# An expert layer's results kept on chip in pairs of experts and combined by one-hot matmuls, with two changes of order ahead of it

## The reference, cut to what matters

```python
x = x + mix @ w_out[l]
h2 = rms_norm(x, norm2_g[l])
# top-1 group of 8 experts, then top-2 experts in it; 32 experts, hidden width 512
for e in range(N_EXPERTS):
    hid = silu(t @ w_gate[e]) * (t @ w_up[e])
    y = y + gates[:, e:e + 1] * (hid @ w_down[e])
x = x + y
```

## Time and profile before

| what | value |
|---|---|
| median of 3 runs | 1212.26 us (1211.14 to 1212.79) |
| profiled execution, its own time | 1212.39 us |
| its span, first to last instruction | 1210.5 us |
| PE busy / PEld busy | 1067.1 us / 693.5 us |
| DVE / ACT / POOL busy | 434.3 / 325.5 / 285.8 us |
| mean granted TensorE clock | 0.955 of 2.4 GHz |
| DMA over the span | 278.12 MB, mean 230 GB/s |

### The profile page before, as it was taken

The page is one execution under the profiler, slowest core; times in us unless marked ns, Lnnn a source line. Parts: engine busy times, 40 slices in busy tenths (PEclk is TensorE's granted clock), DMA queues, the critical chain, the costliest instruction groups (busy, mean ns, idle before and its releaser), DMA issues.

```text
span 1210.5 us, 14085 instructions
## 1 busy us (share of the span) xinstructions
PE 1067.1 (88%) x5550; PEld 693.5 (57%) x5550; DVE 434.3 (36%) x792; ACT 325.5 (27%) x572; POOL 285.8 (24%) x189
## 2 busy tenths in 40 slices
PE   5999999999999999999989599898888878778881
PEld 4779899766698788888868333332333222223320
DVE  3332792699940443469963500100000000000003
ACT  5344632433332655522232111111101011011000
POOL 6333334332333544444330100000000000000002
PEclk8999999999999999999999699999899999998996
DMA  7222242322227222253265889999999999999966
GB/s 178 73 53 72 68 105 71 95 62 70 70 53 243 68 59 64 66 195 104 69 278 200 303 310 411 416 406 414 416 410 417 415 414 403 413 407 416 420 266 215
DMA packets 125966, 278.12 MB, mean 230 GB/s; under 512 B 12688, under 2 KB 98720, under 8 KB 109536
## 3 DMA queue, kind: packets, MB, share of 16 engines
q1 hardware_dynamic: 115584, 254.18, 56.8%
q0 software_dynamic: 4560, 12.83, 3.1%
q10 hardware_dynamic: 5776, 10.49, 2.3%
HBM read 264.95 MB, written 14.62 MB: 231 GB/s over the span
## 4 chain that ended last, share of the span: by engine, by line
PE 61%; DMA 28%; DVE 6%; ACT 2%; issue 2%; SPq 1%; POOL 0%; POOLq 0%; DVEq 0%; ACTq 0%
DMA arena<-w_exp_up_in 24%; PE bank L471 14%; PE bank L492 12%; PE bank L826 11%; PE bank L719 7%; PE bank L839 4%; PE bank L778 3%; DVE work L1295 2%; DMA arena<-w_in_in 2%; PE bank L675 1%; PE bank L658 1%; DMA x_rows<-arena 1%; PE bank L545 1%; DVE piece_r L1408 1%; DVE arena L1297 1%
## 5 line engine op out<-in xcount | busy, mean ns | idle before, releaser
L1671 POOL TENSOR_TENSOR piece_r<-arena,piece_r 128x1024 fp32r<-128x1024 f32 x84 | 201.9, 2410 | 337.4 <-ACT piece_r L903 337.3
L826 PE MATMUL bank<-arena,work 128*64 128x512 f32 x1024 | 240.5, 625 | 40.1 <-DMA arena<-w_exp_up_in 38.9
L471 PE MATMUL bank<-piece_r 128*128 128x512 f32 x936 | 232.5, 399 | 2.3 <-ACT arena L937 2.3
L471 PEld LDWEIGHTS bank<-piece_r 128*128 128x128 f32 x936 | 171.0, 188 | 42.9 <-issue 9.6
L826 PEld LDWEIGHTS bank<-arena,work 128*64 128x64 f32 x1024 | 76.0, 144 | 202.1 <-issue 196.1
L1573 DVE SCALAR_TENSOR_TENSOR work<-bank,slot_rs,work 128x256 f32<-128x256 f32 x32 | 15.5, 484 | 449.2 <-ACT work L1137 449.2
L492 PEld LDWEIGHTS bank<-piece_r 128*128 128x128 f32 x1344 | 162.0, 192 | 6.1 <-issue 6.1
L492 PE MATMUL bank<-piece_r 128*128 128x256 f32 x1344 | 164.9, 284 | 0.0
L839 PE MATMUL bank<-arena,work 128*64 128x512 f32 x512 | 128.5, 648 | 15.1 <-ACT work L1139 15.1
L1735 POOL DMA_INDIRECT arena<-x_rows,idx_all x32 | 29.6, 925 | 461.0 <-PE bank L816 389.5
L903 ACT ACTIVATE piece_r<-arena 128x1024 fp32r<-128x1024 f32 x84 | 88.5, 1056 | 139.0 <-DMA arena<-w_in_in 83.4
(11 more groups left out here) (238 smaller groups left out, 920.7 us busy)
## 6 DMA issues: line engine op xcount, KB each, us to landing
arena<-w_exp_gate_in SPq DMA_DIRECT2D x32, 2048.0 KB, 32.6
arena<-w_exp_up_in SPq DMA_DIRECT2D x32, 2048.0 KB, 39.8
arena<-w_exp_down_in SPq DMA_DIRECT2D x32, 2048.0 KB, 37.9
arena<-w_in_in SPq DMA_DIRECT2D x68, 512.0 KB, 3.9
y_rows<-work ACTq DMA_DIRECT2D x64, 96.0 KB, 6.9
arena<-w_branch_gla_in SPq DMA_DIRECT2D x8, 512.0 KB, 4.1
arena<-w_branch_dsa_in SPq DMA_DIRECT2D x8, 512.0 KB, 5.0
arena<-w_out_in SPq DMA_DIRECT2D x2, 2048.0 KB, 12.5
```

Source lines behind the costliest of these rows:

```text
L471: last = mm(bank[n % 2][:, :], w[:, k, :], h[:, k, :], start=(i == 0 and k == 0), stop=(i == 2 and k == K - 1))
L826: last = mm(bank[0][hf * WIDE:(hf + 1) * WIDE, :], hTe[sl][:, k, :], wgu[sl][2][:, :, k, hf * HALF:(hf + 1) * HALF], start=(k == 0), stop= ...
L1671: Q.tensor_tensor(quarter(w_lo, q), quarter(w_raw, q), quarter(w_hi, q).bitcast(F32), ALU.subtract).then_inc(s["wlo_ready"], 1)
```

## The change

1. **Experts in pairs.** The slots of two experts fill 128 partitions (64 each, 48 used). `idx_pair` has 16 columns, GpSimd issues 16 gathers of 128 rows into two buffers (an unused slot's index is out of bounds and moves nothing). TensorE transposes a pair at a time: eight 128x128 transposes in banks 4 and 7, after the first expert's `gate_up`. VectorE evicts each expert's half in two operations.
2. **Results stay on chip.** A slot's gate weight is multiplied into the hidden product's scale (`slot_sc`). `down` swaps the halves of bank 1 for the second expert of a pair, so that the results of two experts fill 128 partitions for each half of the columns. ScalarE writes their high parts (two copies of 64x512), VectorE their low parts (two subtractions). VectorE makes a one-hot matrix `pick` (slots x 512 tokens) for each half of the columns, by comparison with an iota.
3. **Combine.** For each of 4 blocks of tokens and 2 halves of the columns TensorE multiplies `pick` by the high and then the low part (two fp32r matmuls 128x512) into bank 2, 3 or 6, and VectorE adds the bank to x. Four tiles of the pair before stand in every expert, behind `gate_up` (and the pair's transposes) and ahead of the hidden transposes. The last pair's eight tiles come at the end.
4. **Gone:** `y_rows` with its stores, its zeroing and the two waits for that, and the eight gathers of the end. SP and ScalarE store the output in eight pieces of 256 KB, in turn.
5. **Loops written out** on all engines in the expert stage. The table of extra tiles holds a token and its gate weight.
6. **Mend one:** `split_hi(0)` in place of `split_hi(1)` ahead of the first evictions.
7. **Mend two:** the high passes of output tiles 0 to 3 run first, with k outside; the other passes follow tile by tile. ScalarE's exps are released before the last `place`.

```diff
-            for n in range(2 * T):
-                hf, t = divmod(n, T)
-                for i, (m, w) in enumerate(((mix_hi, wout_hi[hf]), (mix_lo, wout_hi[hf]), (mix_hi, wout_lo[hf]))):
...
+            for k in range(K):
+                for n in range(T):
+                    out_pass(n, 0, [k])
             for n in range(2 * T):
                 hf, t = divmod(n, T)
+                for i in range(1 if hf == 0 else 0, 3):
+                    out_pass(n, i, range(K))
...
             def gather_transposes(b, done):
                 for k in range(K):
-                    last = tr(bank[4][:, k * WIDE:(k + 1) * WIDE], xg[b].rearrange("p (q k) -> p k q", k=K)[0:WIDE, k, :],
-                              ident[0:WIDE, 0:WIDE])
+                    last = tr(bank[4 + k // 4 * 3][:, k % 4 * P:(k % 4 + 1) * P],
+                              xg[b].rearrange("p (q k) -> p k q", k=K)[:, k, :], ident[:, :])
...
+            def combine_tile(onto, picked, hi, lo, t, done):
+                mm(onto, picked[:, t * P:(t + 1) * P], hi, start=True, stop=False)
+                mm(onto, picked[:, t * P:(t + 1) * P], lo, start=False, stop=True).then_inc(done, 1)
+            def combine(p, hf):
+                pe.wait_ge(s["pick_ready"], 2 * p + hf + 1)
+                pe.wait_ge(s["y_lo_ready"], 4 * p + 4 if hf else 4 * p + 3)
+                for t in range(T):
+                    c = TILES * p + T * hf + t
+                    if c >= 3:
+                        pe.wait_ge(s["x_added"], c - 2)
+                    combine_tile(bank[COMB_BANKS[c % 3]][:, :], pick[hf], y_hi[p % 2][hf], y_lo[p % 2][hf], t, s["comb_ps"])
...
+            for e in range(NE):
+                sl, (p, q) = e % 3, divmod(e, 2)
+                pe.wait_ge(wgu_loaded[sl], 32 * (e // 3 + 1))
+                pe.wait_ge(s["he_ready"], e + 1)
+                gate_up(sl, q, s["gu_ready"])
+                if q == 0 and p + 1 < PAIRS_E:
+                    pe.wait_ge(s["he_ready"], e + 2)
+                    pe.wait_ge(xg_loaded[(p + 1) % 2], 16 * ((p + 1) // 2 + 1))
+                    gather_transposes((p + 1) % 2, s["xg_T"])
+                if p >= 1:
+                    combine(p - 1, q)
+                pe.wait_ge(s["hid_ready"], e + 1)
+                hidden_transposes(s["hidT_ps"])
+                pe.wait_ge(s["hidT_ready"], e + 1)
+                pe.wait_ge(wdn_loaded[sl], 16 * (e // 3 + 1))
+                if e >= 1:
+                    pe.wait_ge(s["y_lo_ready"], 2 * e)
+                down(sl, q, s["y_ready"])
...
+            for hf in range(2):
+                combine(PAIRS_E - 1, hf)
...
-            split_hi(1)
+            split_hi(0)
...
-            act.wait_ge(s["rows_zeroed"], 16)
...
+            def high_parts(b, q, done):
+                for hf in range(2):
+                    half = (hf + q) % 2
+                    rows = slice(half * WIDE, (half + 1) * WIDE)
+                    A(y_hi[b][hf][rows, :], bank[1][rows, :], ACT.Copy).then_inc(done, 1)
...
+            for e in range(NE):
+                p, q = divmod(e, 2)
                 dve.wait_ge(s["silu_ready"], e + 1)
+                V.scalar_tensor_tensor(hid, bank[0][:, HALF:F], slot_sc[:, 1, e:e + 1], silu_g,
                                        ALU.mult, ALU.mult).then_inc(s["hid_ready"], 1)
+                if p + 1 < PAIRS_E:
+                    dve.wait_ge(s["xg_T"], p + 2)
+                    evict_gathered(q, s["he_ready"])
+                if p >= 1:
+                    add_combined(p - 1, q)
+                if q == 1:
+                    for hf in range(2):
+                        V.tensor_scalar(pick[hf], tok_iota, tok_pair[:, hf, p:p + 1], None, ALU.is_equal)\
+                            .then_inc(s["pick_ready"], 1)
+                for hf in range(2):
+                    dve.wait_ge(s["y_hi_ready"], 2 * e + hf + 1)
+                    low_part(p % 2, q, hf, s["y_lo_ready"])
...
+            for p in range(PAIRS_E):
+                if p >= 2:
+                    pool.wait_ge(s["xg_T"], p - 1)
+                gather(p % 2, idx_pair[:, p:p + 1], xg_loaded[p % 2])
```

More of the change, by code:

```diff
@@ L757, in tokens_of_slots @@
                 for k in range(TOP_E):
-                    last = mm(bank[4][0:SLOTS, 0:NE], in_slot[:, t, k, :], tok_of[:, t, k, :],
-                              start=(t == 0 and k == 0), stop=(t == T - 1 and k == TOP_E - 1))
+                    for q in range(2):
+                        last = mm(bank[4][q * WIDE:(q + 1) * WIDE, 0:PAIRS_E], in_slot[:, t, k, :], tok_of[:, t, k, q, :],
+                                  start=(t == 0 and k == 0), stop=(t == T - 1 and k == TOP_E - 1))
                 if t == T - 1:
@@ L800, in _ @@
             tokens_of_slots(T - 1)
-            pe.wait_ge(s["rs_of_ready"], 1)
-            for rows in (slice(0, SLOTS), slice(WIDE, WIDE + SLOTS)):
-                for t in range(T):
-                    for k in range(TOP_E):
-                        last = mm(bank[6][rows, 0:NE], in_slot[:, t, k, :], rs_of[:, k, t, :],
-                                  start=(t == 0 and k == 0), stop=(t == T - 1 and k == TOP_E - 1))
-            last.then_inc(s["slot_rs_ps"], 1)
             for j in range(T):
@@ L833, in hidden_transposes, with down @@
                 last.then_inc(done, 1)
[L835 removed]
+            def down(sl, q, done):
                 for k in range(F // P):
                     for hf in range(2):
[L839 removed]
+                        half = (hf + q) % 2
+                        last = mm(bank[1][half * WIDE:(half + 1) * WIDE, :], hidT[:, k % 2, k // 2, :],
                                   wdn[sl][:, k, hf * 512:(hf + 1) * 512], start=(k == 0), stop=(k == F // P - 1))
@@ L1572, in run_expert, with low_part @@
+            def low_part(b, q, hf, done):
+                half = (hf + q) % 2
+                rows = slice(half * WIDE, (half + 1) * WIDE)
+                V.tensor_tensor(y_lo[b][hf][rows, :], bank[1][rows, :], y_hi[b][hf][rows, :].bitcast(F32), ALU.subtract)\
+                    .then_inc(done, 1)
+            for e in range(NE):
+                p, q = divmod(e, 2)
                 dve.wait_ge(s["silu_ready"], e + 1)
-                V.scalar_tensor_tensor(hid, bank[0][:, HALF:F], slot_rs[:, bass.ds(e, 1)], silu_g,
+                V.scalar_tensor_tensor(hid, bank[0][:, HALF:F], slot_sc[:, 1, e:e + 1], silu_g,
```

449 lines of the change are left out of this document (225 added, 224 removed).

## The result

The changed kernel takes **1153.37 us** (median; 1153.17 to 1153.86) against 1212.53 of the kernel before: ratio 0.9509, 95% interval 0.9494 to 0.9524. The spans of the two profiled executions are 1151.4 and 1210.5 us, so 59.1 us went. The runs further down were taken in several sets, each with the kernel before beside it (medians 1211.85 to 1213.36 us), and a ratio is always to that kernel; between two variants of the changed kernel, differences of some 3 us lie within the ratios' intervals. One execution of all, of the kernel without the zeroing transfer, fell in a slow state (2696.74 us) and is not counted.

A forecast was written before the change was run, and what follows sets the result against it. Bound: the chain runs through TensorE up to 670 us; weight loads set the expert stage, 16.13 us an expert mid-stage. Terms 4.4 + 5.5 - 0.5 + 15.9 + 15.9 = 41.2 off 1212.4 give 1171 us; range 1157 to 1188.

The forecast's parts named there:

- the likeliest case: Whole kernel: weight loads stay the expert stage's bound at 15.58 us an expert; 41.2 us off, 1171 us; chance 0.38.
- Expert stage: DMA side: removing 64 stores takes a load from 16.13 to 15.58 us, gathers' cost unchanged; loads end 15.9 us earlier.
- rival 1: Expert stage: paired gathers also relieve the fullest engines; loads 15.1 us, TensorE the bound at 14.6; 1162 us; chance 0.18.
- TensorE's expert: Expert stage: with the combine added, an expert costs TensorE 7.0 + 3.0 + 0.5 + 0.5 + 3.65 = 14.6 us.
- rival 2: Expert stage: TensorE becomes the bound at a worse pace (clock falls, additions late), 15.2 us an expert; 1177 us; chance 0.2.
- Start: First evictions: ScalarE no longer waits for the second weight quarter's load, evictions begin at about 13.1; gain 4.4 us.
- Zeroing: Removed zeroing of y_rows and its two waits: lie beside TensorE work, so gain nothing.
- Output projection: Output tiles 0 to 3: high passes run first, filling TensorE's wait for the weights' low parts; gain 5.5 us.
- Router and first gather: Before the expert stage: store and gather stay in a row, first gather carries two experts' rows; loss 0.5 us.
- End: After the last down matmul: 27.1 us becomes 11.2, with eight additions of 0.69 and the last store; gain 15.9 us.
- Rival 3: Expert stage: load rate does not rise, the stores' packets only filled holes; 1187 us; chance 0.19.
- rival 4: Expert stage: written-out code is fetched while weights fill the DMA, making the kernel slower, about 1290 us; chance 0.05.

## Why the prediction was wrong

Faster was right. The time was 17.6 us too high, because the likeliest case was not the one that came: it had the loads as the bound of the expert stage at 15.58 us an expert, and they took 15.10, so that TensorE at 14.40 sets most of the stage. The terms, against the 17.9 us of span that were missing:

- **Expert stage, 14.0 of them.** The step that failed is "The gathers (2.6%, 0.42 us) move the same valid rows", so that their cost was taken to stay. The rows are the same, but the narrow form cost 0.5 to 0.7 us an expert beyond its share: in the 12 us behind a pair's gathers the DMA moved 363 to 395 GB/s, with the wide form 417 to 425. The stores were sized well (0.55, measured 0.50). With 15.1 an expert the case is rival 1, which I gave 0.18, with its very number (15.1, TensorE the bound). That number was partly luck: it was 427 GB/s plus the gather's own time, and the mechanism beside it, relief of the fullest engines, is not borne out (two wide gathers with one half of the rows each were nearly as cheap, 15.19). What I held against it, "all engines already show 101%", was no argument: the share counts how long packets last, and they lasted 3% longer for the same bytes. The row that could have told was there: 411 GB/s with gathers and stores, 427 with weights alone.
  The sign that I had named for being wrong, TensorE waiting for no load late in the stage, came: 1.1 us in all.
- **TensorE's expert, within that.** Rival 1 still gave 1162. I had 14.6 an expert and it is 14.40, 6 us over 32. I had added durations of groups, 7.0 and 3.65, whose modelled ends overlap the next group's start; start to start the down matmuls take 3.48 (717.34 to 720.82). The order and the wait that I put into it were right (hidden transposes 2.94 after the gate/up matmuls, 3.0 forecast). The clock didn't fall, so rival 2 was out.
- **Start, 1.9.** The evictions came 5.2 earlier (12.31 against 17.49) where I took 4.4, and I overlooked that TensorE's idle stretch also took the clock down for the matmuls behind it.
- **Zeroing, 2.7.** Costed at nothing as "beside TensorE work". It was beside TensorE, but not beside DMA: it delayed a load that TensorE's stream stood behind. The removal alone gave 2.8 (1.0 to 4.6).
- **Output projection, -0.2**, as predicted (5.5, measured 5.3 in the change and 5.2 alone).
- **Router and first gather, -1.3.** I charged 0.5 and it was 1.8. The named suspect (VectorE's longer work ahead of the eviction) wasn't it: the first gather took 9.62 in place of 8.21, and the gathered rows' transposes 1.94 in place of 1.14 (the granted clock was 0.50 from 662 to 680, so 1.2 GHz; the next pair's eight transposes of the same form took 1.16).
- **End, 0.7.** 16.6 against 15.9, with eight additions at 0.61 where I took 0.69, the duration of one alone.

Together 14.0 + 1.9 + 2.7 - 0.2 - 1.3 + 0.7 = 17.8, of 59.1 - 41.2 = 17.9. Rival 3 (the rate does not rise) and rival 4 (code fetches) are refuted, the latter by the run with only the loops written out and by the changed kernel's TensorE, whose waits all have a releaser. What the Trainium skill says (Runtime: NRT & Kernel Launch, Instruction fetch mechanics) agrees with it: no stall was seen.

## What to carry to other kernels

A DMA share of 100% says that packets are under way, not that bytes go at their best (here 363 and 426 GB/s at the same share): compare the bytes a second with a stretch of the same transfers alone, and take the difference as something that a change can win back. Where two bounds are about level, as the loads and TensorE here, removing work from either gives nothing; test it by taking away one side's work altogether, and look whether the other's last event moves. A transfer that no one waits for still has a price if a load that someone waits for stands behind it in time.

## What the runs showed of the hardware

Gathers in instructions over 48 or 64 partitions, one an expert, make the weights that go meanwhile dearer: 39.0 to 39.4 engine-us a MB in the mean of the stage against 37.8 to 37.9, and 43.9 against 37.9 in the 12 us behind one pair's gathers. The same rows in instructions over 128 partitions do not, even when more than half of their indices are out of bounds. I had expected cost to follow rows and bytes. And the first gather lands in 4.4 us when weight loads keep away, against 9.8 beside them.
